# A decoder layer on one core: the gate-matrix stage reordered, with all chunks of `u` inside its loop

## The reference, cut to what matters

```python
def one_chunk(x_c):
    q = (x_c @ w_q).reshape(PEER_CHUNK, PEER_HEADS, PEER_QDIM)
    ...
    t1, i1 = lax.top_k(s1, PEER_TOPK)          # 16 of 128 sub-keys, twice
    t2, i2 = lax.top_k(s2, PEER_TOPK)
    ...
    top_s, pos = lax.top_k(cand_s, PEER_TOPK)  # 16 of the sums, per head
    ids = jnp.take_along_axis(cand_i, pos, axis=-1)
    gate = jax.nn.softmax(top_s, axis=-1)
    hid = jax.nn.gelu(jnp.einsum('chkd,cd->chk', u[ids], x_c))
    return jnp.einsum('chk,chkd->cd', (gate * hid), v[ids])
```

## Time and profile before

| | |
|---|---|
| median of 3 runs | 1973.86 us (1972.97 to 1977.18) |
| the profiled execution | 1973.14 us |
| its span in the profile | 1971.3 us |
| TensorE busy | 1896.8 us, 96% |
| VectorE busy | 1477.1 us, 75% |
| ScalarE busy | 756.0 us, 38% |
| GpSimd busy | 362.0 us, 18% |

### The profile page before, as it was taken

The page is one execution under the profiler, slowest core; times in us unless marked ns, Lnnn a source line. Parts: engine busy times, 40 slices in busy tenths (PEclk is TensorE's granted clock), DMA queues, the critical chain, the costliest instruction groups (busy, mean ns, idle before and its releaser), DMA issues. The chain is left out here.

```text
span 1971.3 us, 35045 instructions
## 1 busy us (share of the span) xinstructions
PE 1896.8 (96%) x13809; PEld 1657.6 (84%) x13809; DVE 1477.1 (75%) x3142; ACT 756.0 (38%) x1165; POOL 362.0 (18%) x337
## 2 busy tenths in 40 slices
PE   8999999899999899999999998999789999999999
PEld 8999887677854689999999998998668888888887
DVE  5353335766662369999999999999878888888887
ACT  5322445222240234433443343776433333333332
POOL 2001100011100003213331330000433222322221
PEclk9999999999999999999999999999999999999999
DMA  4222101100040348668867974287789999999996
GB/s 160 86 87 74 44 22 65 56 3 3 3 172 32 132 132 328 241 235 331 312 236 256 345 278 144 87 268 217 253 336 361 338 337 338 349 337 338 338 339 249
DMA packets 176116, 407.25 MB, mean 207 GB/s; under 512 B 16848, under 2 KB 100048, under 8 KB 175312
## 3 DMA queue, kind: packets, MB, share of 16 engines
q1 hardware_dynamic: 133040, 255.96, 37.9%
q0 software_dynamic: 39744, 144.72, 19.4%
q10 hardware_dynamic: 3168, 4.33, 0.6%
HBM read 358.77 MB, written 46.14 MB: 205 GB/s over the span
## 5 line engine op out<-in xcount | busy, mean ns | idle before, releaser
L89 PE MATMUL eo_ps<-vh,e_wh 128*128 128x512 f32 x768 | 300.3, 391 | 8.7 <-DVE e_wl L2062 8.7
L90 PE MATMUL eo_ps<-vh,e_wl 128*128 128x512 f32 x768 | 299.7, 390 | 0.0
L91 PE MATMUL eo_ps<-vl,e_wh 128*128 128x512 f32 x768 | 299.7, 390 | 0.0
L2028 POOL DMA_INDIRECT e_rows<-in_v,gidx x128 | 140.3, 1096 | 386.3 <-DVE e_acc_t L2042 352.7
L1651 POOL DMA_INDIRECT g_stage<-in_u_rows,gidx x112 | 135.5, 1210 | 391.4 <-DVE gidx L1746 236.8
L2011 ACT CAST vh<-vraw 128x1024 fp32r<-128x1024 f32 x96 | 100.7, 1049 | 235.2 <-PE eo_ps L91 230.2
L89 PE MATMUL h_ps<-x2h,h_uh 128*128 128x384 f32 x520 | 181.2, 348 | 8.4 <-DVE h_ul L1507 5.3
L89 PEld LDWEIGHTS eo_ps<-vh,e_wh 128*128 128x128 f32 x768 | 144.8, 189 | 40.2 <-DVE vl L2053 5.6
L1503 ACT ACTIVATE h_hid<-h_ps 128x384 f32<-128x384 f32 x128 | 63.5, 496 | 290.6 <-PE h_ps L91 209.5
L91 PE MATMUL h_ps<-x2l,h_uh 128*128 128x384 f32 x520 | 174.9, 336 | 0.0
L89 PE MATMUL h_ps<-x2h,q_uh 128*128 128x384 f32 x504 | 170.6, 339 | 4.5 <-ACT h_hid L1503 4.5
(11 more groups left out here) (318 smaller groups left out, 4304.0 us busy)
## 6 DMA issues: line engine op xcount, KB each, us to landing
vraw<-in_v SPq DMA_DIRECT2D x96, 512.0 KB, 6.2
g_stage<-in_u SPq DMA_DIRECT2D x63, 512.0 KB, 6.6
h_uraw<-in_u SPq DMA_DIRECT2D x45, 512.0 KB, 5.4
wraw<-in_w_z SPq DMA_DIRECT2D x43, 512.0 KB, 3.5
HID_scratch<-h_hid SPq DMA_DIRECT2D x106, 192.0 KB, 4.0
e_hid<-HID_scratch SPq DMA_DIRECT2D x96, 192.0 KB, 6.6
G_scratch<-g_stage SPq DMA_DIRECT2D x16, 1024.0 KB, 12.0
g_hot<-in_v SPq DMA_DIRECT2D x32, 512.0 KB, 6.3
```

Of the source, the lines that this page charges most:

```text
L89: nc.tensor.matmul(out, a[0], b[0], start=start, stop=False)
L90: nc.tensor.matmul(out, a[1], b[0], start=False, stop=False)
L91: return nc.tensor.matmul(out, a[0], b[1], start=False, stop=stop)
L2028: nc.gpsimd.indirect_dma_start(rows[:, j % GBUF_E], None, d["v"].rearrange("c p n -> (c p) n"), bass.IndirectOffsetOnAxis(ap=gidx[:, j:j + ...
```

## The change

In the retrieval, the splits of chunks 2 and 3 and the gelus of chunks 0 and 1 move ahead of the copies of the first queries and scores (`AHEAD` = 2). ScalarE's split of chunk 106 moves from the start of the gate stage to the end of the retrieval.

In the gate stage, the product of chunk 106 comes ahead of the first step. The eighths of all other chunks lie in the steps by the table `FILL`: 3 and 2 in turn in the first tile (80), and 11 per eight steps in the second and third (44 each). `begins` and `ends` are the steps in which a chunk's product starts and ends. Chunk i + 1 is split, by ScalarE before its copy and by VectorE after its one-hots, in the step in which chunk i begins. The 16 gathers go out from the stage's start, two ahead of the first load and three behind each load; the dots come in steps 4 to 30. Clears of used semaphores move from the second norm to the block before it, and there are 86 in place of 45. Three buffers of the experts are allocated in another order.

```diff
@@ peer_retrieval, ScalarE
             act.wait_ge(keep["h2_stored"], 16 * NQ)
+            for m in range(AHEAD):
+                split_hi(act, m + 2)
+                gelu(act, m)
             for b in range(2):
                 copy_q(0, b)
...
-                    if m >= 1:
+                    if m > AHEAD:
                         gelu(act, m - 1)
-                    split_hi(act, m + 2)
+                    if m >= AHEAD:
+                        split_hi(act, m + 2)
...
+            split_hi(act, NRC)
@@ gate_matrix
+    REST = NCHUNK - NRC
+    FILL = ((3, 2), (2, 1, 1, 1, 2, 1, 1, 2), (2, 1, 1, 1, 2, 1, 1, 2))
+    quota = [FILL[n // NS][n % len(FILL[n // NS])] for n in range(STEPS)]
+    step_of = [-1] * KD + [n for n in range(STEPS) for _ in range(quota[n])]
+    step_of = (step_of + [STEPS] * (REST * KD))[0:REST * KD]
+    begins = [step_of[i * KD] for i in range(REST)]
+    ends = [step_of[i * KD + KD - 1] for i in range(REST)]
+    dot_step = [4 + j * 7 // 4 for j in range(TOPK)]
@@ gate_matrix, GpSimd
-            for m in range(NRC + GSLOT, TAIL + GSLOT + 1):
-                load(pool, m)
-            pool.wait_ge(g_stored[1], 8 * 16)
...
+            for j in itertools.islice(gathers, 2):
+                gather(j)
+            for m in range(NRC + GSLOT, NCHUNK):
                 load(pool, m)
+                for j in itertools.islice(gathers, 3):
+                    gather(j)
@@ gate_matrix, VectorE, after the one-hots of step n
-                if n % 4 == 3 and n // 4 <= BESIDE:
-                    split_lo(dve, NRC + n // 4)
...
+                if n == 0:
+                    split_lo(dve, NRC + 1)
+                if n in begins[0:REST - 1]:
+                    split_lo(dve, NRC + begins.index(n) + 1)
+                for j in range(TOPK):
+                    if dot_step[j] == n:
+                        dve.wait_ge(rows_in[j], 16)
...
@@ gate_matrix, TensorE
+            fill(-1)
             for n in range(STEPS):
-                if 4 <= n < 4 + 4 * BESIDE:
-                    i = n % 4
-                    product(pe, NRC + n // 4 - 1, range(i * KD // 4, (i + 1) * KD // 4))
+                fill(n)
                 pe.wait_ge(hot1_made, (n + 1) * TB)
...
-            for m in range(TAIL, NCHUNK):
-                product(pe, m)
+            fill(STEPS)
@@ gate_matrix, ScalarE, before the copy of step n
-                if n % 4 == 0 and n // 4 <= BESIDE:
-                    split_hi(act, NRC + n // 4)
+                if n in begins[0:REST - 1]:
+                    split_hi(act, NRC + begins.index(n) + 1)
+                if tile == 1 and i == 0:
+                    act.wait_ge(dotted, TOPK)
```

More of the change, by code:

```diff
@@ L694, in sem @@
         def sem(name):
[L695 removed]
+            s = ctx.enter_context(nc.semaphore(name))
+            keep["spent"].append(s.num)
+            return s
         tanh_w = sb("tanh_w", [HD, T])
@@ L1254, in _ @@
                 sp.dma_start(keep["H2"][:, i], acc[:, i]).then_inc(keep["h2_stored"], 16)
+        @block.gpsimd
+        def _(pool):
+            for n in keep["spent"]:
+                pool.sem_clear(range(n, n + 1))
         @block.tensor
@@ L1681, in _ @@
                 split_w(0, b)
+            for m in range(AHEAD):
+                split_lo(dve, m + 2)
             for h in range(PH):
@@ L1839, in gate_matrix @@
         second = sb("stage", [P, NK, P])
-        stage = (keep["stage"], second)
+        stage = (keep["stage"], second, keep["stage"])
         rows = second[:].rearrange("p (j a) t -> p j (a t)", j=TOPK)
@@ L1853, in _ @@
                 sp.wait_ge(staged, NS * (tile + 1))
-                for r in range(8):
+                for r in range(GPARTS):
                     a = slice(r * QA, (r + 1) * QA)
@@ L1857, in _ @@
                                  stage[tile][:, a]).then_inc(g_stored[tile], 16)
-            for b in range(2):
-                sp.wait_ge(g_stored[b], 8 * 16)
+            for tile in range(ND - 1):
+                sp.wait_ge(g_stored[tile], GPARTS * 16)
             sp.wait_ge(placed, STEPS)
@@ L1890, in _, with fill @@
                                             ALU.is_equal, ALU.mult).then_inc(hot1_made, 1)
-                if n % 4 == 3 and n // 4 <= BESIDE:
-                    split_lo(dve, NRC + n // 4)
[L1893 to L1901, removed]
+                if n == 0:
[5 more added lines that the diff above has]
+                        dve.wait_ge(rows_in[j], 16)
+                        nc.vector.tensor_tensor_reduce(rows[:, j], rows[:, j], x2t[:], 1.0, 0.0, ALU.mult, ALU.add,
+                                                       hdot[:, LATE + j:LATE + j + 1]).then_inc(dotted, 1)
+            for i in range(REST):
+                if begins[i] == STEPS and i + 1 < REST:
+                    split_lo(dve, NRC + i + 1)
         @block.tensor
         def _(pe):
+            def fill(n):
+                for i in range(REST):
+                    ks = [k for k in range(KD) if step_of[i * KD + k] == n]
+                    if ks:
+                        product(pe, NRC + i, ks)
+            fill(-1)
             for n in range(STEPS):
-                if 4 <= n < 4 + 4 * BESIDE:
-                    i = n % 4
-                    product(pe, NRC + n // 4 - 1, range(i * KD // 4, (i + 1) * KD // 4))
+                fill(n)
                 pe.wait_ge(hot1_made, (n + 1) * TB)
@@ L1915, in _ @@
                 mm.then_inc(placed, 1)
[L1916 to L1917 removed]
+            fill(STEPS)
         @block.scalar
         def _(act):
+            split_hi(act, NRC + 1)
             for n in range(STEPS):
                 tile, i = n // NS, n % NS
[L1923 to L1924 removed]
+                if n in begins[0:REST - 1]:
+                    split_hi(act, NRC + begins.index(n) + 1)
+                if tile == 1 and i == 0:
+                    act.wait_ge(dotted, TOPK)
                 if tile == 2 and i == 0:
[L1926 removed]
+                    act.wait_ge(g_stored[0], GPARTS * 16)
                 act.wait_ge(placed, n + 1)
[L1928 removed]
+                nc.scalar.copy(stage[tile][:, :, i * TB:i * TB + TB].rearrange("p a t -> p t a"),
                                ps[:, n % NBANK]).then_inc(staged, 1)
[L1930 to L1937, removed]
+                if n in ends or n == 0:
+                    gelu(act, NRC + (ends.index(n) if n > 0 else 0))
+                    store(act, NRC + (ends.index(n) if n > 0 else 0))
+            for i in range(REST):
+                if begins[i] == STEPS and i + 1 < REST:
+                    split_hi(act, NRC + i + 1)
+                if ends[i] == STEPS:
+                    gelu(act, NRC + i)
+                    store(act, NRC + i)
 def experts(nc, d, keep):
```

35 lines of the change are left out of this document (19 added, 16 removed).

## The result

| | before | changed |
|---|---|---|
| median | 1974.01 us | 2028.04 us (2025.11 to 2030.3, 4 runs) |
| ratio, with its 95% interval | | 1.027 (1.0252 to 1.0288) |
| span of the profiled execution | 1971.3 us | 2027.1 us |

A forecast was written before the change was run, and what follows sets the result against it. VectorE's work was taken to bound the gate stage, forecast at 267 us against 214.0 (+53 us); with -6 us at the retrieval's start, 1971.3 + 53 - 6 = 2018 us of span, given as 2019 us, range 1994 to 2050.

The forecast's parts named there:

- VectorE bounds the stage, so filling TensorE's holes gives nothing: Gate stage: VectorE has 200 us of work before and after, TensorE 177 us, so filling holes does not shorten it.
- The wait that the change adds: Gate stage loop: VectorE's split waits for ScalarE's high half, 19 times 2.2 us, 42 us, bounds 30 and 63.
- the sign: Gate stage: VectorE's split waits for ScalarE's high half some 20 times, 40 to 50 us in total.
- waits above 1.58 us: Gate stage loop: waits exceed this lower bound where fills delay TensorE's placing, up to 3.3 us; 2.2 us taken.
- The stage's start and end: Gate stage: 6.7 us wait for chunk 108's load; at the end 1.2 us, then 7.5 us TensorE idleness instead of 5.3.
- The clock: Gate stage: TensorE idles at each chunk; five clock falls of 1.5 us on the chain, 8 us, bounds 0 and 29.
- The retrieval's start: Retrieval: TensorE's 4.46 us wait ahead of chunk 2's product and a 1.5 us clock fall go, -6 us.
- The clears: Block before the second norm: 86 semaphore clears in place of 45 fit into GpSimd's idle time and cost nothing.
- VectorE does not wait in the loop: Rival, chance 0.08: no added wait in the gate stage loop; stage 217 us, kernel 1971 us.
- the clock falls at every chunk: Rival, chance 0.15: in the gate stage, falls cost 29 us in place of 8, so 2040 us or more.
- the waits are at their lower bounds and the clock holds: Rival, chance 0.18: loop waits 30 us, start 4.2, no clock falls; stage 245 us, kernel 1998 us.
- the start's gain does not carry through: Rival, chance 0.05: the retrieval's gain at its start is lost before the end; kernel 2025 us.

The follow-up runs named there:

- the repetition: The changed kernel run again unchanged, as the reference for its variants on the same chip: 2025.72 us, ratio 1.0263 to the kernel before.
- group 1: Runs on one chip, kernel before 1983.82 us; two traces: kernel before with only `AHEAD` = 2, 1978.85 us, or low half in the high half's step, 2021.71 us.
- the last version: The changed kernel with VectorE's low half two steps later, and chunk 106's product filling steps 0 to 2: 1963.5 us, ratio 0.9939 to the kernel before.

## Why the prediction was right

- **VectorE bounds the stage, so filling TensorE's holes gives nothing: right.** With the waits gone and the new table kept the stage is 214.9 us, with the old one 214.0.
- **The wait that the change adds: right, and shown by itself**, by taking it out of the changed kernel and by putting it into the kernel before. Its size, 42 us, came out as 47.2. With the first wait it is 53.4 us, over the 40 to 50 us named as the sign; TensorE's wait for one-hots came to 56.4 us where about 70 were named, and the experts' first matmul at 1496 where 1485 was. The reason given for waits above 1.58 us was half wrong. I named fills ahead of the placing; I did not see that the gelu and store of the chunk that ends in step n - 1 stand ahead of the cast of step n, in ten of nineteen cases. They were in ScalarE's rows of the change that stand ahead of the prediction. With them moved the loop's waits are 31.8 us, near the lower bound of 30, though three of them lie below 1.58 us by the dots of the step before.
- **The stage's start and end: right**, 6.2 for 6.7 and 8.8 for 8.7 us. But the end's extra 2 us did not stay: TensorE's waits for the experts' operands are 8.9 us in all, against 8.7 before, probably since the later loads had landed meanwhile. Behind the first matmul that is 1.6 us in place of 3.4, most of the 2.4 us by which the experts are shorter; it is read from waits, and was not tried.
- **The clock: the mis-sized term, and partly luck.** "Five falls on the chain, 8 us" were 14 phases at the lower clock, 13 in the repetition. Taken away by spare work they are worth 11.5 us of time, and 13.6 to 16.2 us of the stage. That is 1.0 to 1.1 us for a fall, measured on one chip, and not 1.5. So I had the falls too few by more than half, and each too dear; the two errors partly cancel, and the term looks better than its reasons. I also left out that a slow phase holds ScalarE's copy and the cast behind it, where VectorE waits. The two terms overlap, so they can't be added: with the clock held, the loop's waits are 40.0 us.
- **The retrieval's start: right**, -6 us forecast, 5 to 6 us measured (5 by the times, 5.9 by the two traces of group 1), with TensorE's wait ahead of the product of chunk 2 gone. The clears show nothing: TensorE's idleness ahead of the first product of `u`, behind them, is 3.08 and 2.23 us in two traces of the kernel before and 2.15 and 3.14 us in two of the changed one. They and the order of the experts' buffers were not tried alone.
- **The rivals.** That VectorE does not wait in the loop is out for the change as made; two steps more of distance make it true, and its sum, 217 us for the stage, measured 214.9. That the clock falls at every chunk came nearer in number than the forecast, 14 falls in a loop of nineteen such waits, but its price did not: 11.5 us where it had 29. That the waits are at their lower bounds and the clock holds is out by 47.2 us for 30 and by the falls; that the start's gain does not carry through is out by the 5 us above.

## What to carry to other kernels

When two engines share the two halves of one piece of work, the distance in steps between the halves is what counts: read the chain from one to the other once, and keep the second engine's own work between the halves longer than that chain. Count every instruction that the first engine does between its release and its half, also those of other pieces. Where one engine has the most work of a stage, work put into another engine's holes gains little: nothing with the new table here, 2 us with the last version. A wait of that engine costs more than its own length where it lets TensorE's clock fall: 11.5 us of the loss here.

## What the runs showed of the hardware

- **The length of the idle time alone does not tell whether the clock falls.** Behind 2.37 us of idleness it was at 0.50 within the placing (1241.58); behind 3.42 us it stayed at 1.00 (the placing at 1373.20 took 1.16 us). Of 21 placings that waited, 14 had a fall, and seven had none. The Trainium skill, "TensorE: Matmul & The Clock Gate", section "Why this matters for your kernels", warns of idle gaps between bursts; the trace agrees that gaps of this size can take the clock down, and shows that they don't always.
- **The clock can fall when TensorE is already at work again.** At five of the 14 it fell 1.0 to 1.5 us behind the start of the placing, so the first matmuls behind a gap ran at full pace and the next at half: 1.16 us for the placing at 1298.51, 1.91 us for the one at 1301.00.
- **198 spare matmuls, 49 us of TensorE's time, made the kernel 11.5 us faster**, by holding the clock at 0.99 where it was 0.90 in the repetition on the same chip.
- **VectorE stood still beside a GpSimd instruction**: 3.16 us in place of 1.11, and so at all eight halves that GpSimd made.
- **One gather held GpSimd for 13.41 us, in another trace 11.78 us**, where the sixteen took 1.25 us each in the kernel before's first trace. Both ended 0.8 us behind VectorE's last one-hots. In that first trace eleven of the sixteen went out beside one-hots too and none was long; why is open. The two long ones are of one chip.
